# A decoder layer on one core: first projections from a transposed copy of x, with the norm factor applied behind them

## What is computed

```python
xn = rms_norm(h, attn_norm)                   # h * rsqrt(mean(h*h) + eps) * gain
qm, km, vm, qs, ks_, vs = split(xn @ w_in, 6)
qm, km = rms_norm(qm, q_norm), rms_norm(km, k_norm)      # per head
o_m = softmax attention(qm, km, vm, relative bias)
o_s = stick-breaking attention(qs, ks_, vs)
h = h + concat(rms_norm(o_m), rms_norm(o_s)) @ w_out
h = h + peer_ffn(rms_norm(h, ffn_norm))       # 16384 single-neuron experts
h = h + sigmoid(rms_norm(h, ple_norm) @ w_gate) * (p @ w_ple)
```

## Time and profile before

| | |
|---|---|
| median of 3 runs | 983.71 us (982.79 to 984.46) |
| the profiled execution | 982.79 us, span 981.1 us |
| TensorE busy | 963.4 us, 98% of the span |
| VectorE, ScalarE, GpSimd busy | 69%, 63%, 34% |
| HBM read | 167.45 MB, 172 GB/s over the span |
| TensorE clock granted | 0.998 of full |

### The profile page before, as it was taken

One profiled execution on the slowest core, in us unless ns is written; L12 is line 12 of the kernel. 1 busy time (PEld: TensorE's weight loads), 2 busy tenths in 40 slices (PEclk: granted clock), 3 DMA queues, 4 the chain that ended last, 5 costly groups with the idle time before them and its releaser, 6 DMA issues.

```text
span 981.1 us, 19103 instructions
## 1 busy us (share of the span) xinstructions
PE 963.4 (98%) x6234; PEld 876.3 (89%) x6234; DVE 680.2 (69%) x1377; ACT 619.4 (63%) x1026; POOL 333.7 (34%) x152
## 2 busy tenths in 40 slices
PE   8999989999999999999999999999999999999998
PEld 5887879999999999999999998888888888888877
DVE  6636663999935888888888884666655555667663
ACT  6477554266665888888888885555555555566643
POOL 0002020088887777777777773000000000012000
PEclk9999999999999999999999999999999999999999
DMA  8563422045554444444444445555567777555511
GB/s 313 215 221 122 174 89 87 1 151 181 183 181 167 168 159 164 164 157 171 152 169 158 163 163 181 193 192 193 193 234 236 236 251 230 194 194 192 191 61 43
DMA packets 43803, 168.94 MB, mean 172 GB/s; under 512 B 5075, under 2 KB 6524, under 8 KB 42492
## 3 DMA queue, kind: packets, MB, share of 16 engines
q1 hardware_dynamic: 43392, 168.46, 49.5%
q10 hardware_dynamic: 380, 0.07, 0.0%
HBM read 167.45 MB, written 1.06 MB: 172 GB/s over the span
## 4 chain that ended last, share of the span: by engine, by line
PE 82%; POOL 7%; DVE 5%; issue 4%; ACT 1%; DMA 1%; POOLq 0%; SPq 0%; DVEq 0%; ACTq 0%
PE pair L1410 12%; PE pair L1407 12%; PE pair L1409 12%; PE bank L1119 11%; PE bank L1121 11%; PE bank L1120 11%; POOL t_lo L1082 7%; PE pair L1369 3%; PE pair L1144 2%; PE pair L1145 2%; PE pair L1146 2%; DVE w_lo L667 1%; PE pair L1450 1%; PE pair L1452 1%; PE pair L1451 1%
## 5 line engine op out<-in xcount | busy, mean ns | idle before, releaser
L1082 POOL TENSOR_TENSOR t_lo<-t_raw,t_hi 128x1024 fp32r<-128x1024 f32 x130 | 312.3, 2412 | 153.0 <-ACT t_hi L519 152.9
L519 ACT ACTIVATE t_hi<-t_raw 128x1024 fp32r<-128x1024 f32 x256 | 270.5, 1057 | 80.1 <-DMA t_raw<-v_chunks 56.0
L1119 PE MATMUL bank<-xt_hi,t_hi 128*128 128x256 f32 x1024 | 290.1, 283 | 2.0 <-POOL t_lo L1082 2.0
L1120 PE MATMUL bank<-xt_lo,t_hi 128*128 128x256 f32 x1024 | 289.8, 283 | 0.0
L1121 PE MATMUL bank<-xt_hi,t_lo 128*128 128x256 f32 x1024 | 289.8, 283 | 0.0
L820 DVE TENSOR_TENSOR t_lo<-t_raw,t_hi 128x1024 fp32r<-128x1024 f32 x126 | 154.7, 1228 | 100.1 <-ACT t_hi L519 99.9
L1407 PE MATMUL pair<-t_hi,g_hi 128*128 128x512 f32 x512 | 199.2, 389 | 0.0
L1409 PE MATMUL pair<-t_lo,g_hi 128*128 128x512 f32 x512 | 199.2, 389 | 0.0
L1410 PE MATMUL pair<-t_hi,g_lo 128*128 128x512 f32 x512 | 199.2, 389 | 0.0
L1119 PEld LDWEIGHTS bank<-xt_hi,t_hi 128*128 128x128 f32 x1024 | 196.5, 192 | 2.4 <-POOL t_lo L1082 2.4
L1120 PEld LDWEIGHTS bank<-xt_lo,t_hi 128*128 128x128 f32 x1024 | 196.6, 192 | 0.0
(11 more groups left out here) (246 smaller groups left out, 1304.4 us busy)
## 6 DMA issues: line engine op xcount, KB each, us to landing
t_raw<-u_chunks SPq DMA_DIRECT2D x128, 512.0 KB, 3.3
t_raw<-v_chunks SPq DMA_DIRECT2D x128, 512.0 KB, 3.3
w_raw<-w_in SPq DMA_DIRECT2D x4, 2048.0 KB, 8.4
w_raw<-w_query SPq DMA_DIRECT2D x4, 2048.0 KB, 7.7
w_raw<-w_in SPq DMA_DIRECT2D x8, 512.0 KB, 8.8
w_raw<-w_out SPq DMA_DIRECT2D x2, 2048.0 KB, 7.8
wg_raw<-w_gate SPq DMA_DIRECT2D x8, 512.0 KB, 4.7
h<-x SPq DMA_DIRECT2D x2, 512.0 KB, 4.3
```

The lines of the kernel that those rows point to most:

```text
L519: nc.scalar.activation(t_hi[:, q % RING, :], t_raw[:, q % RING, :], ACT.Copy).then_inc(t_hi_ready, 1)
L1082: nc.gpsimd.tensor_tensor(t_lo[:, q, :], t_raw[:, q, :], t_hi[:, q, :].bitcast(f32), ALU.subtract).then_inc(t_lo_pool, 1)
L1119: mm(dst, ah, bh, start=(c == 0), stop=False)
L1120: mm(dst, ah, bl, start=False, stop=False)
```

## The change

A second copy of x, transposed on the host, is a new input: `x_t`, 128 partitions x 8 chunks x 256 tokens. The first products use x_t times the gain, without the norm factor. The factor (one per token) is applied later: ScalarE's copies of Q_M and K_M out of PSUM take it as their scale, VectorE's copies of the values too; for Q_S and K_S, where tokens lie along the row, TensorE makes a row of the negated factors (two products with a diagonal matrix, behind K_M), ScalarE copies it, and VectorE multiplies the products by it on their way out of PSUM (in place of ScalarE's copies).

The queues: ScalarE issues x_t piece 0 and the gains only. SP issues two chunks of group 0, then x_t pieces and the rest of group 0 in turn, the four quarters of group 1, x, the constants, the QK gains and the two inputs of the bias table, and then group 2 in two halves by columns, runs of 1 KB. ScalarE squares x behind the splits of group 1, and makes the table's copy behind the inverse of the root. The 16 transposes of x are gone.

The diff, cut to its core:

```diff
@@ sync
+            for c in range(2):
+                sp.dma_start(w_raw[:, 0, c, :], w_in[0, :, c, :]).then_inc(piece_loaded[c], 16)
+            for b in range(1, 4):
+                sp.dma_start(xt_raw[:, 2 * b:2 * b + 2, :], x_t[:, 2 * b:2 * b + 2, :]).then_inc(xt_loaded[b], 16)
+                sp.dma_start(w_raw[:, 0, 2 * b:2 * b + 2, :], w_in[0, :, 2 * b:2 * b + 2, :]
+                             ).then_inc(piece_loaded[b + 1], 16)
+            for b in range(4):
+                sp.dma_start(w_raw[:, 1, 2 * b:2 * b + 2, :], w_in[1, :, 2 * b:2 * b + 2, :]
+                             ).then_inc(quarter_loaded[b], 16)
             for tt in range(TT):
                 sp.dma_start(h[:, tt, :], x[tt * P:(tt + 1) * P, :]).then_inc(x_loaded[tt], 16)
             sp.dma_start(cst[:, :, :], consts).then_inc(small_loaded, 16)
...
+            sp.dma_start(qkg[:, :], qk_gain).then_inc(small_loaded, 16)
+            sp.dma_start(tab_in[:, 0:TAB], bucket_onehot).then_inc(tab_loaded, 16)
+            sp.dma_start(tab_in[0:REL, TAB:TAB + NH], rel_bias).then_inc(tab_loaded, 16)
...
-            load_group(2)
+            sp.wait_ge(*split(0))
+            for k in range(2):
+                m = slice(256 * k, 256 * (k + 1))
+                sp.dma_start(w_raw[:, 0, :, m], w_in[2, :, :, m]).then_inc(half_loaded[k], 16)
             sp.wait_ge(tab_copied, 1)
@@ scalar
+            act.dma_start(xt_raw[:, 0:2, :], x_t[:, 0:2, :]).then_inc(xt_loaded[0], 16)
+            act.dma_start(gain[:, :, :], gains).then_inc(gain_loaded, 16)
             nc.scalar.preload_act_table(ACT.Sqrt)
+            act.wait_ge(gain_loaded, 16)
+            for b in range(4):
+                act.wait_ge(xt_loaded[b], 16)
+                for c in (2 * b, 2 * b + 1):
+                    ins = nc.scalar.activation(xt_hi[:, c, :], xt_raw[:, c, :], ACT.Copy, scale=gain[:, 0, c:c + 1])
+                ins.then_inc(xt_hi_ready, 1)
+                for c in (2 * b, 2 * b + 1):
+                    act.wait_ge(piece_loaded[c if b == 0 else b + 1], 16)
+                    nc.scalar.activation(w_hi[:, 0, c, :], w_raw[:, 0, c, :], ACT.Copy).then_inc(quarter_hi, 1)
...
+            act.wait_ge(inverse_ready, 1)
             act.wait_ge(tab_made, 1)
             nc.scalar.copy(tab_out[:, :], bank[0][0:NH, 0:TAB]).then_inc(tab_copied, 1)
             out_of_psum(Q_M)
-            split_group(2)
+            for k in range(2):
+                m = slice(256 * k, 256 * (k + 1))
+                act.wait_ge(half_loaded[k], 16)
+                if k == 0:
+                    act.wait_ge(*used(0))
+                nc.scalar.activation(w_hi[:, 0, :, m], w_raw[:, 0, :, m], ACT.Copy).then_inc(half_hi, 1)
             out_of_psum(K_M)
+            act.wait_ge(row_made, 1)
+            nc.scalar.activation(rstd_row[:, :], bank[1][:, 0:SEQ], ACT.Copy, scale=-SCALE).then_inc(row_ready, 1)
             split_group(3)
             act.wait_ge(qk_mean, 1)
             nc.scalar.activation(QRSTD, QSS, ACT.Sqrt).then_inc(qk_root, 1)
-            out_of_psum(Q_S)
...
-            out_of_psum(K_S)
@@ vector
+            for c in range(DC):
+                dve.wait_ge(xt_hi_ready, c // 2 + 1)
+                nc.vector.scalar_tensor_tensor(out=xt_lo[:, c, :], in0=xt_raw[:, c, :], scalar=gain[:, 0, c:c + 1],
+                                               in1=xt_hi[:, c, :].bitcast(f32), op0=ALU.mult,
+                                               op1=ALU.subtract).then_inc(xt_lo_ready, 1)
+                dve.wait_ge(quarter_hi, c + 1)
+                nc.vector.tensor_tensor(w_lo[:, 0, c, :], w_raw[:, 0, c, :], w_hi[:, 0, c, :].bitcast(f32),
+                                        ALU.subtract).then_inc(quarter_lo, 1)
...
+            dve.sem_inc(inverse_ready, 1)
+            dve.wait_ge(small_loaded, 32)
+            for tt in range(TT):
+                ins = nc.vector.tensor_scalar(diag[:, P * tt:P * (tt + 1)], ident, norm_stats(0)[2][:, tt:tt + 1], None,
+                                              ALU.mult)
+            ins.then_inc(diag_ready, 1)
...
             split_group(3)
+            dve.wait_ge(row_ready, 1)
+            columns_scaled(Q_S)
             split_group(4)
+            columns_scaled(K_S)
             split_group(5)
@@ tensor
-            pe.wait_ge(small_loaded, 48)
-            transposes(0, 0)
             for c in range(DC):
                 pe.wait_ge(xt_lo_ready, c + 1)
-                pe.wait_ge(quarter_lo, c // 2 + 1)
+                pe.wait_ge(quarter_lo, c + 1)
...
             rows_group(K_M, 6)
+            pe.wait_ge(diag_ready, 1)
+            for tt in range(TT):
+                ins = mm(bank[1][:, P * tt:P * (tt + 1)], neg_ones, diag[:, P * tt:P * (tt + 1)], start=True, stop=True)
+            ins.then_inc(row_made, 1)
             pe.wait_ge(group_out, 2)
             columns_group(Q_S, 4)
...
             pe.wait_ge(qk_normed, TT)
             pe.wait_ge(tab_copied, 1)
+            pe.wait_ge(row_ready, 1)
+            pe.wait_ge(small_loaded, 32)
```

More of the change, by code:

```diff
@@ L69, with layer_program @@
 OUT0, QUERY0, N_GROUPS = 6, 8, 12
-def layer_program(nc, x, p_t, rel_bias, bucket_onehot, consts, gains, qk_gain, w_in, w_out, w_query,
+def layer_program(nc, x, x_t, p_t, rel_bias, bucket_onehot, consts, gains, qk_gain, w_in, w_out, w_query,
                   subkeys_t, u_chunks, v_chunks, w_gate, w_ple, out):
@@ L152, in layer_program @@
         warm = tile("warm", [P, 512], ZONE + 4 * 10240)
+        xt_raw = tile("xt_raw", [P, DC, SEQ], where["xt_lo"])
+        diag = tile("diag", [P, SEQ], ZONE + 4 * 10752)
+        rstd_row = tile("rstd_row", [P, SEQ], ZONE + 4 * 11008)
         t_raw = tile("t_raw", [P, RING, D], ZONE)
@@ L381, in out_of_psum @@
                 act.wait_ge(*used(n))
-                b = 4 if n in (Q_M, Q_S) else 6
+                b = 4 if n == Q_M else 6
                 for q in range(2):
[L384 to L394, removed]
-            nc.scalar.preload_act_table(ACT.Sqrt)
+                    nc.scalar.activation(qk_nat[:, q, NH * n:NH * (n + 1), :].rearrange("p a b -> p (a b)"),
+                                         bank[b + q][:, :], ACT.Copy,
+                                         scale=norm_stats(0)[2][:, q:q + 1]).then_inc(group_out, 1)
+            act.dma_start(xt_raw[:, 0:2, :], x_t[:, 0:2, :]).then_inc(xt_loaded[0], 16)
+            act.dma_start(gain[:, :, :], gains).then_inc(gain_loaded, 16)
+            nc.scalar.preload_act_table(ACT.Sqrt)
+            act.wait_ge(gain_loaded, 16)
[7 more added lines that the diff above has]
+                    nc.scalar.activation(w_hi[:, 0, c, :], w_raw[:, 0, c, :], ACT.Copy).then_inc(quarter_hi, 1)
+            for b in range(4):
+                act.wait_ge(quarter_loaded[b], 16)
+                nc.scalar.activation(w_hi[:, 1, 2 * b:2 * b + 2, :], w_raw[:, 1, 2 * b:2 * b + 2, :],
+                                     ACT.Copy).then_inc(quarter_hi, 1)
             for tt in range(TT):
@@ L694, in _ @@
+            for b in range(4):
+                dve.wait_ge(quarter_hi, DC + b + 1)
+                nc.vector.tensor_tensor(w_lo[:, 1, 2 * b:2 * b + 2, :], w_raw[:, 1, 2 * b:2 * b + 2, :],
+                                        w_hi[:, 1, 2 * b:2 * b + 2, :].bitcast(f32),
+                                        ALU.subtract).then_inc(quarter_lo, 1)
             for tt in range(TT):
                 mean(0, tt + 1, tt, tt + 1, D)
+            for tt in range(TT):
                 link(inverse(0, tt + 1, tt, tt + 1))
-                scaled(0, tt)
@@ L717, in _, with columns_scaled @@
                 nc.vector.tensor_tensor(qk_nat[:, tt, :, :], qk_nat[:, tt, :, :], r, ALU.mult).then_inc(qk_normed, 1)
+            def columns_scaled(n):
+                dve.wait_ge(*used(n))
+                b = 4 if n == Q_S else 6
+                for q in range(2):
+                    g = 4 * (n - Q_S) + 2 * q
+                    nc.vector.tensor_tensor(qkt_s[:, g:g + 2, :], bank[b + q][:, :].rearrange("p (a t) -> p a t", a=2),
+                                            rstd_row[:, :].unsqueeze(1).to_broadcast([P, 2, SEQ]),
+                                            ALU.mult).then_inc(columns_out, 1)
             split_group(3)
+            dve.wait_ge(row_ready, 1)
+            columns_scaled(Q_S)
             split_group(4)
+            columns_scaled(K_S)
             split_group(5)
@@ L1136, in columns_group @@
             def columns_group(n, b):
-                pe.wait_ge(*split(n))
                 for q in range(4):
+                    if n == Q_S and q % 2 == 0:
+                        pe.wait_ge(half_lo, q // 2 + 1)
+                    elif q == 0:
+                        pe.wait_ge(*split(n))
                     m = slice(P * q, P * (q + 1))
@@ L1305, in _ @@
             pe.wait_ge(h1_ready, 2)
-            transposes(2, TT)
+            transposes(2, 0)
             def key_scores(n):
@@ L1492 @@
         "x": a["x"].reshape(SEQ, D),
```

(1 more changed line is left out.)

44 lines of the change are left out of this document (23 added, 21 removed).

## The result

| | median of the runs | ratio to before (95%) | profiled execution: time, span, clock |
|---|---|---|---|
| before | 984.11 us (982.79 to 986.29, 16 runs) | | 982.79, 981.1, 0.998 |
| after | 985.82 us (985.04 to 987.67, 16 runs) | 1.0018 (1.0011 to 1.0026) | 987.06, 985.4, 0.993 |

The forecast was 0.1 us faster; it is 1.7 us slower, inside the range and on the other side of no change. The two profiled executions stand at opposite ends of their spreads (before's is the fastest of its 16 runs, after's the second slowest), so the 4.3 us between their spans are not the change's 1.7. This matters for all that follows: the medians price, the traces only explain.

The account below looks back on a forecast made before the run. TensorE was taken to bound the kernel, with group 3's landing a second chain of 1.00 us slack ahead of K_S. K_S -0.2 and +0.1 for a copy sum to -0.1 us: median 983.6, range 981.3 to 986.2.

Parts of the forecast that it names:

- Part 2: Bias-table product: its inputs, last on SP's queue, usable at 19.9; TensorE waits 1.0, K_M starts 2.5 us earlier at 20.65.
- Part 3: Group 3's landing behind store and skew load: usable at 36.9, 0.8 later than before; K_S at 48.0 against 48.24.
- Part 1: The start: without transposes and norm ahead of it, the first product comes at 7.8, 3.5 us earlier.
- My count of packets: SP's queue ahead of the table product: packets priced by size, 276 engine-us or 17.3 us, table's inputs in at 19.5.
- the 38.5 that I had named as a sign of being wrong: Group 3's split on ScalarE: forecast to begin at 36.9; beginning before 35 or after 38.5 would mean wrong.
- Part 4: Small edits: norm row's products 0.5 us of TensorE, hidden; columns_scaled 0.68 a copy, 0.1 us lost at K_S.
- Rival (c): TensorE's clock falls behind its idleness ahead of K_S, K_S's first products at half pace: +2.7, 986.3; chance 0.07.
- An equal gap was harmless: Argument against the clock's fall: before's gap from warm-up's end to 11.33 had full-pace products after it.
- Rival (b): 1 KB packets cost what the skew's do: group 2's halves take 8.5, K_S 2.4 later, 986.0; chance 0.10.
- Rival (a): Queue faster than counted, group 3 lands by 34.7, K_S at 45.8: whole gain of 2.3, 981.4; chance 0.13.
- Rival (d): First products start no earlier as gains or chunk 0 land late; K_M stays near 23, 983.6 to 984; chance 0.05.

Follow-up runs that it names:

- e0_after: The changed kernel again, nothing edited, for another trace: 986.0 us, ratio 1.0017; its profiled execution was its fastest, 983.5.
- e1: The changed kernel with the bias table's two inputs back on ScalarE's queue behind the gains: 986.23 us, ratio 1.0021 to before.
- e5: e1 with group 2 as one transfer of large runs instead of two halves in 1 KB runs: 985.39 us, ratio 1.0009 to before.
- e3: The changed kernel with four products on zeros ahead of TensorE's wait for the table's inputs: 985.36 us, ratio 1.0013 to before.
- e12: The changed kernel with twelve small products filling TensorE's gap between transposes near 140 us: 984.05 us, ratio 0.9999 to before.
- e0b_after: The changed kernel once more, nothing edited, for a third trace: a single execution, 987.07 us.
- e11: The kernel before with twelve small products filling TensorE's gap between transposes near 140 us: 982.62 us, ratio 0.9985 to before.
- e2: e1 with group 3 also issued ahead of the wait for the table's copy, store and skew load: 981.52 us, ratio 0.9974 to before.
- e7: The kernel before with group 3 issued ahead of the table's store: 983.85 us, ratio 0.9998 to before.
- e4: The changed kernel with group 3 issued ahead of the table's store, table's inputs still last on SP's queue: 984.99 us, ratio 1.0019 to before.
- e8: e2 with group 2 as one transfer of large runs instead of two halves: 981.66 us, ratio 0.9977 to before.
- e9: e4 with four products on zeros ahead of TensorE's wait for the table's inputs: 983.9 us, ratio 0.9997 to before.
- e10: e2 with twelve small products filling TensorE's gap between transposes near 140 us: 979.62 us, ratio 0.9955 to before.

## Why the prediction was wrong, point by point

Two steps failed, both on when a transfer is usable: Part 2 had the table's inputs at 19.9 (measured 21.6 to 22.6), and Part 3 had the skew load issued at 26.0 and group 3 usable at 36.9 (measured 27.1 and 38.3 in e0_after, later in the other profiles of after). The second turns the forecast -0.2 us at K_S into +1.05, and it is enough to keep the time up: e1, where the first is gone, is no faster than after.

**Part 1 (start) held.** Gains landed 4.0 us after their issue, first product at 7.59 for a forecast 7.8.

**Part 2 (table product) failed first in time.** "The table's inputs are in at 19.5, usable at about 19.9": they were usable at 21.6 in the fastest profile of after (e0_after) and at 22.6 in the other two. TensorE waited 1.06 to 3.65 us for a forecast 1.0. A part can be read: from 2 to 8 us the queue moved 1.68 MB where before it moved 2.00, though all 16 engines count as busy, as in these windows of after:

```profile
5.00:6.00 1.00, 1.00 (x3) 0.34 (x1) 0.00 (x0) 0.70 (x2) 0.00 (x0) 1.00 1.02 219
6.00:7.00 1.00, 0.40 (x1) 0.00 (x0) 0.73 (x2) 1.00 (x3) 0.00 (x0) 1.00 0.89 223
```

0.32 MB at the later 415 GB/s is 0.8 us. My count of packets gave every engine its full pace from 2.3 us on. The larger part lies behind the bytes. Summed over windows of half a us, the 6.6 MB that stand ahead of group 2's halves have moved by about 20.0 in after and 19.9 in e0_after, and TensorE could use the table's inputs 2.6 and 1.7 us later. The second half of x, just ahead of them (6.3 MB in all, by about 19.1), is used from 21.10 and 20.45, also 1.4 to 2.0 us behind its turn. These are estimates, as the engines don't finish in step. So a landing told late, as in Part 3, is the likelier reason; a share for group 2's first half, which runs at the same time (325 GB/s in 20 to 22 us, where its runs alone reach 340 to 350), is not excluded by any run.

**Part 3 (group 3) had the mechanism right and its start wrong.** Price of a 1 KB packet: in 24 to 26 us only such runs flow, 340 GB/s from 16 engines, so 1024 x 16 / 340,000 = 0.048 us, the value taken. "From landing to K_S 11.1 us": 11.0 in e0_after, e1 and e5 alike. From the skew's issue to group 3's use, 10.9 forecast, it was 11.0 to 11.2 (e1, e5, e0_after, e3). "19.5 + 6.1 = 25.6, done 0.4 later at 26.0": here two things failed. The halves' traffic ends at 26.3, 0.7 late (it begins near 20.0 and takes 6.3), and the skew load is issued 1.7 us behind that, as the windows of after show:

```profile
25.00:26.00 1.00, 1.00 (x4) 0.81 (x3) 0.00 (x0) 1.00 (x3) 0.00 (x0) 0.50 1.06 334
26.00:27.00 1.00, 1.00 (x3) 0.74 (x3) 0.00 (x0) 1.00 (x1) 0.00 (x0) 0.50 0.26 86
27.00:28.00 1.00, 1.00 (x4) 0.77 (x3) 0.51 (x1) 0.65 (x2) 0.00 (x0) 0.50 0.02 8
```

The DMA engines do next to nothing from 26.3 to 28.0, and the second half too is used only from 27.81. In e0_after the traffic ends at 26.2 and the skew is issued at 27.11. Between the bounds of 0.4 and 1.4 for the store's end I had taken the lower, since "the issue's own latency is hidden"; it was 0.9 and 1.7. In both the engine that waits goes on well behind the last byte, and being queued early hid none of that. Group 3 was usable at 38.29 in e0_after, 38.80 in e1 and 39.04 in e12 instead of 36.9, in the last two past the 38.5 that I had named as a sign of being wrong (in after the split began at 39.39 without a wait for it). In e0_after it made K_S 1.05 us later (49.29 against 48.24) where the forecast had -0.2: 1.25 of the miss of 1.8. The other 0.6 is not traced to a place.

**Part 4 held.** The norm row's products cost 0.36 us (37.53 to 37.89) for 0.5. They are hidden where group 3's landing sets K_S (e0_after, e1), and not where TensorE itself is late (after, e0b_after, e12). columns_scaled took 0.64 us a piece for 0.68.

**Rival (c) was dismissed on a bad argument.** "An equal gap was harmless" in before's profile was one execution; in e11, before's kernel with a fill far behind, the mean clock shows a fall in 4 of 11, and in the profiled one of them it stands during Q_M. And its place was too narrow: I looked for the fall at K_S only, while the wait that I had myself put ahead of the table product stands between two dense stretches. Its size was right where the fall is the long one: forecast +2.7, measured K_M 13.65 - 11.03 = +2.6. The Trainium skill, "TensorE: Matmul & The Clock Gate" (HAM oscillation), says that gaps between bursts throttle the engine again; the trace agrees now, 3.42 us of idleness with 0.50 behind it, and shows falls behind shorter idle times too (1.96 us ahead of Q_M in e0_after, 2.65 near 140 us). **Rival (b)** did not come (0.048). **Rival (a)** did not come, though e2 shows what it would have been worth: the medians differ by 984.17 - 981.52 = 2.65 us, for 2.3 forecast. **Rival (d)** did not come as described, since the first product is 3.7 us earlier; K_M stayed near 23 all the same in the first profile, by the wait for the table.

The sum as it should have been: K_S +1.05 where the clock falls early or not at all (the landing sets it), +2.9 to +3.6 where it falls behind the table (51.18, 51.76 and 51.82 against 48.24); before's own start pays a fall in some executions too (50.09 in e11). Net +1.4 (e12 - e11), with 0.3 more near 140 us that may be noise. By the mean clocks of e12 the median belongs to the executions with a short fall, so to the first kind if that fall is the early one; in which place it lies in executions without a profile isn't seen.

## What to carry to other kernels

When a start is made earlier, follow it to the second chain first: here the serial piece of store, wait and reload stood ahead of a load that did not need it, and moving that load (two lines) together with two tiny transfers was worth 4.3 us where the rewritten start alone lost 1.7. A small transfer that TensorE needs does not belong at the end of a queue of large ones, and a wait of 3 us between dense products can cost its length and then nearly as much again in clock (here 3.42 and 2.6 us), where nothing later hides it. Where one kernel's times spread over 3 us, one profile is a sample: take several before saying that a gap is harmless.

## What the runs showed of the hardware

Every profile, with TensorE's idle time ahead of the first product and of the table product, and where the granted clock stood under 1.00 up to 56 us (from the timelines and 1 us windows, to about a us). In before, e7 and e11 the 16 transposes stand between the warm-up and Q_M, so the first column is the idle time behind them; in the others it is the idle time behind the warm-up:

| profile | idle ahead of Q_M | ahead of the table | clock fallen in |
|---|---|---|---|
| before, e7 | 1.29, 1.41 | 0, 0 | nowhere |
| e11 (before + fill) | 1.70 | 0 | 12 to 16 us |
| after, e0b_after, e12 | 1.20, 1.33, 1.80 | 3.42, 3.65, 3.10 | 22 to 29 us, 21 to 28 in e12 |
| e0_after, e4 | 1.96, 2.01 | 1.06, 0.87 | 8 to 12 us |
| e2, e8 | 2.13, 2.00 | 0, 0 | 8 to 12 us |
| e5 | 2.31 | 0 | 8 to 12 and 49 to 53 us |
| e1 | 1.77 | 0 | 49 to 53 us |
| e3, e9 (products while waiting) | 0.81, 0.87 | 0, 0 | nowhere |
| e10 | 1.60 | 0 | nowhere |

I had not expected that behind a wait of 1.96 to 2.31 us after the warm-up some 3.5 us run at the 1.2 GHz level, in all five profiles that have it, and behind one of 3.1 to 3.65 us ahead of the table seven. Where the wait after the warm-up was 0.81 to 1.80 us there was no early fall. That this wait decides which place is hit is not shown: three profiles of after fit it (1.20, 1.33 and 1.96 us), and an early fall also shortens the later wait by making Q_M slower. One more warm-up product may close it; that was not tried.

Near 140 us an idle time of 2.65 us between short transposes has a fall in it or right behind it in each trace without the fill, 3.4 us long in three and 6.8 in nine. Before (timeline, then windows), and the same place in after:

```profile
139.71 1.56 PE L1106 MATMUL bank<-cst,xs 128*128 128x128 f32 x8 [2.65 <-DVE xs L682]
```

```profile
140.00:142.00 2.00, 1.58 (x9) 1.21 (x8) 0.94 (x3) 1.81 (x6) 0.00 (x0) 0.55 0.52 221
142.00:144.00 2.00, 2.00 (x12) 2.00 (x12) 2.00 (x6) 2.00 (x5) 0.00 (x0) 0.60 0.00 0
144.00:146.00 2.00, 2.00 (x19) 2.00 (x18) 0.28 (x1) 2.00 (x1) 0.00 (x0) 1.00 0.00 0
```

```profile
142.00:144.00 2.00, 0.69 (x3) 0.69 (x4) 0.95 (x3) 0.20 (x1) 0.00 (x0) 0.54 1.01 434
144.00:146.00 2.00, 1.74 (x8) 1.37 (x8) 1.09 (x3) 1.96 (x6) 0.00 (x0) 0.50 0.33 139
146.00:148.00 2.00, 2.00 (x11) 2.00 (x11) 2.00 (x6) 2.00 (x4) 0.00 (x0) 0.50 0.00 0
148.00:150.00 2.00, 2.00 (x15) 2.00 (x14) 0.13 (x1) 2.00 (x1) 0.00 (x0) 0.75 0.00 0
```

The fill took it away in every profile of e10, e11 and e12, and with it 1.5 us of before's median (984.13 to 982.62) and 1.9 of e2's. What makes it 3.4 or 6.8 us long stays open, as does why the DMA engines are slow from 5 to 7 us.
